# The norm spread, the gram, the value rows, the turned matrix and the turned output placed one level later in TensorE's order in the recurrent periods of a two-layer encoder trunk

## What is computed

```python
a_mat = jnp.where(strict, jnp.einsum('bhnid,bhnjd->bhnij', kb, k) * decay, 0.0)
rhs = jnp.concatenate([v * beta[..., None], kb * jnp.exp(g)[..., None]], axis=-1)
sol = lax.linalg.triangular_solve(a_mat + eye, rhs, left_side=True, lower=True, unit_diagonal=True)
u, w = sol[..., :dv], sol[..., dv:]
attn = jnp.einsum('bhnid,bhnjd->bhnij', q, k) * decay
def step(state, inp):
    q_c, k_c, u_c, w_c, g_c, attn_c = inp
    v_new = u_c - jnp.einsum('bhcd,bhde->bhce', w_c, state)
    o_c = (jnp.einsum('bhcd,bhde->bhce', q_c * jnp.exp(g_c)[..., None], state)
           + jnp.einsum('bhij,bhje->bhie', attn_c, v_new))
    g_last = g_c[..., -1:]
    state = (state * jnp.exp(g_last)[..., None]
             + jnp.einsum('bhcd,bhce->bhde', k_c * jnp.exp(g_last - g_c)[..., None], v_new))
    return state, o_c
```

## Time and profile before

| | |
|---|---|
| median of three executions | 2410.43 us (2410.15 to 2412.61) |
| the profiled execution's own time | 2418.84 us |
| its span, first to last instruction | 2416.8 us |
| TensorE busy | 2355.4 us, 97% of the span |
| VectorE busy | 1692.5 us, 70% |
| ScalarE busy | 1020.2 us, 42% |
| GpSimd busy | 541.6 us, 22% |
| mean granted TensorE clock | 0.981 |
| chain that ended last | PE 89%, DVE 6%, ACT 3% |

### The profile page before, as it was taken

The page is one execution under the profiler, slowest core; times in us unless marked ns, Lnnn a source line. Parts: engine busy times, 40 slices in busy tenths (PEclk is TensorE's granted clock), DMA queues, the critical chain, the costliest instruction groups (busy, mean ns, idle before and its releaser), DMA issues.

```text
span 2416.8 us, 33785 instructions
## 1 busy us (share of the span) xinstructions
PE 2355.4 (97%) x12922; PEld 1856.2 (77%) x12922; DVE 1692.5 (70%) x2670; ACT 1020.2 (42%) x1804; POOL 541.6 (22%) x501
## 2 busy tenths in 40 slices
PE   9999999998999999999999999989999999999998
PEld 6587777874568788888888877766878888888887
DVE  5389986877856787777765587637678776766557
ACT  5323323655654433333343445447443333333344
POOL 5015533431100043433340000000005343332000
PEclk9999996998999999999999999999999999999999
DMA  6121110010033354545596631111335554558663
GB/s 184 53 79 44 37 42 2 3 37 1 27 96 88 126 196 164 172 153 173 179 311 212 193 104 44 48 40 36 89 128 194 166 172 155 170 182 307 208 193 129
DMA packets 236271, 298.26 MB, mean 123 GB/s; under 512 B 13424, under 2 KB 175232, under 8 KB 227024
## 3 DMA queue, kind: packets, MB, share of 16 engines
q1 hardware_dynamic: 220848, 207.66, 27.9%
q0 software_dynamic: 15264, 88.45, 9.8%
HBM read 206.95 MB, written 88.60 MB: 122 GB/s over the span
## 4 chain that ended last, share of the span: by engine, by line
PE 89%; DVE 6%; ACT 3%; issue 1%; POOL 0%; DVEq 0%; ACTq 0%; POOLq 0%
PE ps L376 25%; PE ps L378 24%; PE ps L377 24%; PE ps L3111 1%; PE ps L3099 1%; PE ps L3131 1%; ACT d_p L1721 1%; PE ps L2447 1%; PE ps L2461 1%; PE ps L2456 1%; DVE met L2212 1%; PE ps L2499 1%; PE ps L1994 1%; PE ps L1948 1%; PE ps L2516 1%
## 5 line engine op out<-in xcount | busy, mean ns | idle before, releaser
L376 PE MATMUL ps<-uhi,whi 128*128 128x512 f32 x608 | 244.9, 403 | 7.9 <-DVE ulo L535 3.3
L376 PE MATMUL ps<-q_T,whi 128*128 128x512 f32 x640 | 249.2, 389 | 1.6 <-ACT upr L860 1.6
L378 PE MATMUL ps<-q_T,wlo 128*128 128x512 f32 x640 | 249.0, 389 | 0.0
L377 PE MATMUL ps<-q_T,whi 128*128 128x512 f32 x640 | 249.0, 389 | 0.0
L376 PE MATMUL ps<-q_B,whi 128*128 128x512 f32 x608 | 238.9, 393 | 2.4 <-DVE q_B L535 2.4
L376 PE MATMUL ps<-ahi,whi 128*128 128x512 f32 x616 | 240.4, 390 | 0.0
L378 PE MATMUL ps<-ahi,wlo 128*128 128x512 f32 x616 | 239.7, 389 | 0.0
L377 PE MATMUL ps<-alo,whi 128*128 128x512 f32 x616 | 239.7, 389 | 0.0
L378 PE MATMUL ps<-uhi,wlo 128*128 128x512 f32 x608 | 237.0, 390 | 0.0
L377 PE MATMUL ps<-ulo,whi 128*128 128x512 f32 x608 | 237.0, 390 | 0.0
L378 PE MATMUL ps<-q_B,wlo 128*128 128x512 f32 x608 | 236.7, 389 | 0.0
(11 more groups left out here) (476 smaller groups left out, 5083.9 us busy)
## 6 DMA issues: line engine op xcount, KB each, us to landing
wraw<-in_ffn_w_gate_dram SPq DMA_DIRECT2D x44, 512.0 KB, 5.0
wd<-in_ffn_w_down_dram POOLq DMA_DIRECT2D x22, 1024.0 KB, 7.1
w_sums<-wd POOLq DMA_DIRECT2D x22, 1024.0 KB, 5.0
wraw<-w_sums SPq DMA_DIRECT2D x40, 512.0 KB, 3.8
araw<-act_sums SPq DMA_DIRECT2D x40, 512.0 KB, 4.7
wraw<-in_ffn_w_down_dram SPq DMA_DIRECT2D x30, 512.0 KB, 5.9
araw<-acts SPq DMA_DIRECT2D x30, 512.0 KB, 6.6
wraw<-in_ab_w_in_dram SPq DMA_DIRECT2D x24, 512.0 KB, 3.8
```

The source lines that it names most:

```text
L376: nc.tensor.matmul(dst, wh, xh, start=start, stop=False, **kw)
L377: nc.tensor.matmul(dst, wh, xl, start=False, stop=False, **kw)
L378: return nc.tensor.matmul(dst, wl, xh, start=False, stop=stop, **kw)
```

## The change

In each recurrent period five pieces of TensorE's program are written one step of the level chain later: `spread_norms` behind X of level 0, `gram` behind X of level 2, `value_rows` behind P of level 3, `turn_a` behind P of level 4, `turn_out` behind X of level 4. ScalarE's `copy_a` goes behind its copy of level 4, VectorE's `masks` behind its subtraction of level 0, and VectorE's `value_rows` behind the third place of the search. No instruction is added or removed.

```diff
--- before.py
+++ after.py
@@ -2531,12 +2531,12 @@
                     level_p(n + 1, 0)
                 if S_:
                     through_state((n, 0), (n - 1, 1) if O_ else None)
-                if A_:
-                    spread_norms(n + 2)
                 if n == NB - 1:
                     heads(pe, 0)
                 if L_:
                     level_x(n + 1, 0)
+                if A_:
+                    spread_norms(n + 2)
                 if n == NB - 2:
                     value_half(pe, 0)
                 if A_:
@@ -2561,22 +2561,20 @@
                     level_p(n + 1, 2)
                 if n == NB - 2:
                     value_half(pe, 3)
+                if L_:
+                    level_x(n + 1, 2)
                 if A_:
                     gram(n + 2)
-                if L_:
-                    level_x(n + 1, 2)
                 if n == NB - 2:
                     value_half(pe, 4)
+                if L_:
+                    level_p(n + 1, 3)
                 if A_:
                     value_rows(n + 2)
-                if L_:
-                    level_p(n + 1, 3)
                 if n == NB - 2:
                     value_half(pe, 5)
                 if L_:
                     level_x(n + 1, 3)
-                if A_:
-                    turn_a(n + 2)
                 if S_:
                     through_state((n, 1), (n, 0))
                 if n == NB - 1:
@@ -2584,15 +2582,16 @@
                 if L_:
                     level_p(n + 1, 4)
                 if A_:
+                    turn_a(n + 2)
                     key_rows(n + 2)
                 if n == -2:
                     key_norm_sums(pe)
                 if n == -1:
                     key_norm_spread(pe)
+                if L_:
+                    level_x(n + 1, 4)
                 if O_:
                     turn_out(pe, n - 1)
-                if L_:
-                    level_x(n + 1, 4)
                 if S_:
                     add_state(n, 1)
                 if L_:
@@ -2778,8 +2777,6 @@
                     w_high(act, Tile(first[("ab_out", 0)] + 1))
                 if O_:
                     normed_out(act, n - 1)
-                if A_:
-                    copy_a(n + 2)
                 if S_:
                     new_values(n, 1)
                 if n == NB - 1:
@@ -2787,6 +2784,7 @@
                 if L_:
                     level(n + 1, 4)
                 if A_:
+                    copy_a(n + 2)
                     rows(n + 2, 0)
                 if L_:
                     copy_w(n + 1)
@@ -2973,10 +2971,10 @@
 
             for n in range(-2, NB):
                 S_, L_, A_, O_ = 0 <= n, n + 1 in range(NB), n + 2 < NB, n >= 1
+                if L_:
+                    level(n + 1, 0)
                 if A_:
                     masks(n + 2)
-                if L_:
-                    level(n + 1, 0)
                 if n == NB - 2:
                     value_half_move(dve, 0, dve.tensor_copy)
                 if n == -1:
@@ -3005,10 +3003,11 @@
                     add_state(n, 0)
                 if A_:
                     weigh_gram(n + 2)
-                    value_rows(n + 2)
                 if O_:
                     invert(dve, n - 1)
                 search(n, 2)
+                if A_:
+                    value_rows(n + 2)
                 if L_:
                     level(n + 1, 3)
                 search(n, 3)
```

## The result

| | before | changed |
|---|---|---|
| median of six executions beside each other | 2412.03 us (2410.15 to 2418.15) | 2427.12 us (2423.22 to 2439.34) |
| ratio, 95% interval | | 1.0071 (1.0041 to 1.0101) |
| profiled execution, span | 2418.84, 2416.8 | 2437.96, 2435.9 |
| mean granted clock | 0.981 | 0.975 |

The account below looks back on a forecast made before the run. TensorE was taken as the stage's bound; 0.95 + 0 + 0.35 + 0.10 - 0.45 + 0.45 = +1.4 us on the median 2410.43 gave 2411.8 us, range 2404 to 2417.

Parts of the forecast that it names:

- What bounds the kernel: Recurrent stage, 346 to 541 us: TensorE itself is the bound, with 3.4 us waiting for ScalarE and 1.4 for VectorE.
- Level 3's wait given, level 2's taken: Steady periods: value rows cover X of level 3, -0.45 us; X of level 2 loses the gram, +0.45 us.
- The steady period: n = 1 to 5, one P of level 0 to the next: stays at 19.66 us within 0.15 us.
- The 0.07 us: Allowance for slightly different neighbours of the groups, +0.07 us in each of five periods, 0.35 us.
- the 0.10 us: Allowance for the one period whose slowest search steps use up VectorE's margin: +0.10 us.
- VectorE's margin at P of level 4: Steady period: VectorE finishes about 0.3 us before P of level 4 wants its result, so no wait there.
- Period n = 3: P of level 3 still waits about 1.1 us for VectorE; the filled copy wait behind it gives -0.45 us.
- Period n = 6: No preparation; the turned output moves behind X of level 4, leaving that X a bare wait: +0.45 us.
- Periods n = -1 and n = 0: n = -1: three new waits (X of level 0 and 2, P of level 4), one removed, +0.95 us; n = 0: 0.
- The sum of the covers: Covers taken and given across all periods of the stage: +1.4 us in total, counted as no change.
- the clock stays low longer: Rival, 16%: bare waits in n = -1 and n = 0 bring one more 23.7 us low stretch, +10.4 us, 2422.2.
- The clock rises sooner: Rival, 20%: norms and decay back to back raise the clock at about 363 in n = -1; 2404.3 or 2401.4 us.

Follow-up runs that it names:

- turn_alone: Kernel before with only the turned matrix behind P of level 4 and its ScalarE copy behind that of level 4: 2414.94 us, ratio 1.0007.
- norms_alone: Kernel before with only the norms' spread behind X of level 0 and VectorE's masks behind the subtraction of level 0: 2412.96 us, ratio 1.0002.
- middle_back: Changed kernel with the edits of level 2 and 3 (gram, value rows and their scaling) undone, the four others kept: 2425.74 us, ratio 1.0043.
- middle_alone: Kernel before with only gram behind X of level 2 and value rows (with their VectorE scaling) behind P of level 3: 2431.9 us, ratio 1.0056.
- middle_again: The same program as middle_alone, against the kernel before, timed once more on another chip: 2425.41 us, ratio 1.0044.
- middle_fill8: middle_alone with eight dense gram matmuls added between P and X of level 2 in seven periods: 2413.59 us, ratio 1.0001.
- middle_light: middle_alone with sixteen light 64x64x32 matmuls added between P and X of level 2 in seven periods: 2414.24 us, ratio 1.0000.
- middle_light8: middle_alone with eight light matmuls, about as long as the wait, added between P and X of level 2: 2416.59 us, ratio 1.0006.
- fill8: Changed kernel with eight further gram matmuls between P and X of level 2 in seven periods: 2413.28 us, ratio 1.0001.
- before_delay: Kernel before with three further ScalarE copies ahead of the one X of level 3 waits for, lengthening that wait: 2426.24 us, ratio 1.0048.
- gram_alone: Kernel before with only the gram behind X of level 2, value rows left ahead of P of level 3: 2415.9 us, ratio 1.0012.
- middle_delay: middle_alone with three further ScalarE copies ahead of the one X of level 2 waits for: 2425.74 us, ratio 1.0051.
- before_light: Kernel before with eight light matmuls added in its bare wait between P and X of level 3, seven periods: 2414.82 us, ratio 1.0008.

## Why the prediction was wrong, by its own steps

- **What bounds the kernel.** Right: TensorE is the bound in the stage, and its clock was the third thing read there. It turned out to be the first in weight.
- **Level 3's wait given, level 2's taken.** Right in each period: X of level 3 doesn't wait any more, X of level 2 waits 0.37 us at 443.70 and so on, in all seven periods from -1 to 5 (the ten waits of L2456 above are these, X of level 1 in n = -1 and n = 0, and X of level 0 in n = -1). ScalarE was ready in time.
- **The steady period.** Right: the timeline of TensorE from P of level 0 to P of level 0 in n = 5, all at the full clock, goes from 517.20 to 536.86, 19.66 us, where 19.66 within 0.15 had been said. The 0.07 us that the sum took for each of five periods, and the 0.10 us for one of them, do not show there:

```profile
517.20 0.60 PE L2447 MATMUL ps<-g_XX,g_BT 64*64 64x32 f32 x16
...
524.82 0.65 PE L2447 MATMUL ps<-g_XX,g_BT 64*64 64x32 f32 x16
525.85 0.66 PE L2456 MATMUL ps<-g_P,g_XX 64*64 64x32 f32 x16 [0.37 <-ACT g_P L2674]
...
527.92 0.66 PE L2447 MATMUL ps<-g_XX,g_BT 64*64 64x32 f32 x16
528.51 0.66 PE L2418 MATMUL ps<-unit,bT 128*128 128x128 f32 x4
529.09 0.66 PE L2456 MATMUL ps<-g_P,g_XX 64*64 64x32 f32 x16
...
536.86 0.60 PE L2447 MATMUL ps<-g_XX,g_BT 64*64 64x32 f32 x16
```

- **VectorE's margin at P of level 4.** Right for the whole change (no such wait stands in that period). turn_alone shows how narrow it was: there the same P waits 0.41 us.
- **Period n = 3.** P of level 3 waits 1.26 us (about 1.1 forecast, 1.09 before), and its waits together grew by 0.15 us where 0.45 us less had been forecast. The step that failed there: before, the value rows stood ahead of P of level 3, where VectorE's lateness covered them; behind it they cost their 0.59 us, more than the trip of 0.45 us that they fill, and X of level 3 follows P by 1.17 us where it followed by 1.02. Three rows of the changed kernel (P and X of level 2, P of level 3), and P of level 2 of before, which waited just as long:

```profile
474.95 0.65 PE L2447 MATMUL ps<-g_XX,g_BT 64*64 64x32 f32 x16 [0.32 <-DVE g_XX L2886]
475.97 0.66 PE L2456 MATMUL ps<-g_P,g_XX 64*64 64x32 f32 x16 [0.37 <-ACT g_P L2674]
479.38 0.66 PE L2447 MATMUL ps<-g_XX,g_BT 64*64 64x32 f32 x16 [1.26 <-DVE g_XX L2886]
```

```profile
462.55 0.66 PE L2447 MATMUL ps<-g_XX,g_BT 64*64 64x32 f32 x16 [0.34 <-DVE g_XX L2888]
```

- **Period n = 6.** X of level 4 waits 0.39 us, as forecast.
- **Periods n = -1 and n = 0.** The three new waits forecast for n = -1 came (X of level 0 and 2, P of level 4). Two more did not stand in the sum: P of level 0 waits 0.45 us (before, where the clock fell at 352.6 and so ahead of it, it does not), and P of level 2 waits 0.87 us for VectorE where it waited 0.44. The 0.87 us belong to the move of norms and `masks`: norms_alone and middle_back show it too (0.87 and 0.85 us), turn_alone, without that move, 0.44. In n = 0 P of level 3 waits 0.42 us for VectorE, before not. In the timeline (n = -1: P and X of level 0, P and X of level 2, P of level 4; n = 0: P of level 3):

```profile
355.75 1.07 PE L2447 MATMUL ps<-g_XX,g_BT 64*64 64x32 f32 x16 [0.45 <-issue]
357.19 1.07 PE L2456 MATMUL ps<-g_P,g_XX 64*64 64x32 f32 x16 [0.37 <-ACT g_P L2674]
364.93 0.77 PE L2447 MATMUL ps<-g_XX,g_BT 64*64 64x32 f32 x16 [0.87 <-DVE g_XX L2886]
366.06 1.07 PE L2456 MATMUL ps<-g_P,g_XX 64*64 64x32 f32 x16 [0.37 <-ACT g_P L2674]
374.21 1.06 PE L2447 MATMUL ps<-g_XX,g_BT 64*64 64x32 f32 x16 [0.44 <-issue]
396.59 1.07 PE L2447 MATMUL ps<-g_XX,g_BT 64*64 64x32 f32 x16 [0.42 <-DVE g_XX L2886]
```

- **The sum of the covers.** Mis-sized: 2.8 us in the stage (2.6 by the single waits) in place of 1.4. By the waits, n = -1 cost 1.7 us (0.95 forecast), n = 0 cost 0.4 (0), n = 3 cost 0.15 (-0.45), the steady periods nothing (0.45) and n = 6 0.4 (0.45). At one clock, .981, the changed kernel took 2423.6 us and before 2418 to 2419, so up to 5 us may be plain in the timed executions.
- **The step that failed: the clock.** The forecast took the clock for unchanged, and gave "the clock stays low longer" 16% and one further stretch of 23.7 us, 10.4 us. Its test came out as written (over 11 us more at 0.50), and its idea, that moved bare waits bring the clock down, is the right one. Its place and size are not. It looked to n = -1 and n = 0, where the changed kernel has no more time at 0.50 than before (47.4 us in the three windows shown, 50.9 before). The low clock came with 41 us more, 18.0 us, and in steady periods, where the argument against it ("the steady periods each had a wait of their own and kept 1.00 for 51.0 us") had looked for safety. That argument treated one bare wait as good as another. Before, the wait stood at level 3, right behind gram and value rows; the change puts it at level 2, and the first of the long new stretches begins right there, as do all three of middle_alone's in the steady periods.
- **The clock rises sooner.** Given 20%. The clock did come up at 361.9, about where the rival put it (363), but was down again at 365.4, and norms_alone gained nothing over its executions.

What the runs show of the cause: moving gram and value rows together is enough for most of the loss (middle_alone, middle_again); filling the bare wait of level 2 undoes it, with dense or with light work (middle_fill8, middle_light, mostly middle_light8; in the whole change fill8); lengthening the wait that the kernel before has brings a loss of the same size by the same way (before_delay). So with gram and value rows both moved, the small idle beside the 64x64 matmuls of level 2 is a needed part of the cause: with it the seven periods cost some 13 us or more, filled 1 to 4 us. That such an idle is enough by itself is not shown, and gram_alone, which has it too, speaks against it.

The Trainium skill (TensorE: Matmul & The Clock Gate, Part 1, on a second failure mode) tells of a kernel in which TensorE idles for moments between groups of matmuls, often enough that it goes back and forth between the two clocks and loses throughput by the changes. The trace agrees with it: idles of 0.37 us, and 95.6 us at 1.2 GHz in five stretches. It doesn't say why the clock stays low for long with one order and comes back soon with another: gram_alone has sixteen such idles and a clock of .9849.

What stays open: why the clock comes back so much sooner in gram_alone than in middle_alone, with more waits; why the four other edits do it together (middle_back) where norms and turned matrix alone don't and the turned output does little; why middle_delay was no worse than middle_alone; and why before_light gained nothing.

## What to carry to other kernels

Where a stage runs on small matmuls and its windows already show both clocks, a wait of a few tenths of a microsecond that only changes its place need not be free: read the granted clock ahead of the waits, and price a move by further stretches at the low clock in several periods, not one. A little work without use in such a wait can be worth more than it takes (in middle_fill8 189.5 less 183.1 us, 0.9 us in each of seven periods, and the kernel 12 to 18 us shorter; in the kernel before, before_light, it gained nothing), and it is the quickest test of whether the clock is the cause. Time such a kernel often enough to see the whole spread of its executions, since one trace is one draw.

## What was not expected of the hardware

- The executions of one program differ by 18 us with the clock: middle_alone took 2413.71 us at .984, 2425 at .978 and 2432 at .975. Within middle_alone that is 2.0 us for each 0.001 of mean clock; straight lines through the executions of the other kernels give 1.1 to 2.4 us.
- More work on the engine that is the bound made the kernel faster: 56 dense matmuls more took the changed kernel from 2427.1 to 2413.3 us.
- The long stretches at 0.50 in the steady periods run without any idle (27.20 us busy of 27.20 at 443.90, 20.40 of 20.40 at 481.50): once the clock is low the waits that seem to have brought it down are gone, as everything else on the path keeps its speed, and the clock still stays low.
